# A hybrid attention and MLP step on 8 cores: staging of late input tiles, exponentials over two key tiles of both maps, and score bursts in halves

## The chip, the cores and the metric

One Trainium2 chip, a program on all 8 of its cores. Each core works on its own part: two prompts of 256 tokens and one half (1024 tokens) of a latent sequence of 2048, whose keys and values it computes in full. The metric is the device time in microseconds of the slowest core.

## The reference

One layer, run over context tokens (modulated by c_ctx) and latent tokens (modulated by c):

```
h = rms_norm(x) * (1 + scale) + shift          # scale, shift from silu(c) @ w_ada
q, k, v, u, g = split(h @ w_in)                # 1024 columns each
q, k = rms_norm per 64 (and rotary, latent tokens only)
a = softmax(q1 k1^T / 8) - lam * softmax(q2 k2^T / 8)   # 8 heads, two maps each
att = rms_norm(a @ v);  sgu = gelu(u) * (w_s @ layer_norm(gelu(g)) + b_s)
y = x + g1 * (concat(att, sgu) @ w_o)
y = y + g2 * (relu(h2 @ w_ff1)^2 @ w_ff2)      # h2: modulated norm of y
```

Context queries see the 256 keys of their own prompt; latent queries see 2048 latent keys and 256 cached ones. The keys and values of the context tokens are outputs too.

## The kernel before, in words

A core has 12 tiles of 128 tokens of its own (0 to 3 context, 4 to 11 latent) and 8 tiles (12 to 19, "late") of the other half of the sequence, which need only keys and values. Heads are handled in pairs, p = 0 to 3.

**How the order is made.** The program is written by a planner (class Sched). Work is described by generators ("threads") with priorities; a small model of the engines' costs, of PSUM banks and of the DMA rate decides when each posted operation is issued, and that order becomes the fixed order of each engine's instructions. Semaphore waits are added from the data dependences alone. So an event (Ev), a pool (Pool) or a delay in the planner sets where an instruction stands in its engine's queue; on the chip it then waits only for its data. A lower number is a higher priority.

**Start.** Modulation weights (ada, 8 units u of 4 parts) stream in through POOL's DMA queue, with weights of the projections and the input tiles x. norm_x(tt) squares a tile on ACT, takes the inverse root, scales it into xn and gives its x buffer back. The projections of the own tiles for pair 0 (k, q, v) and pair 1 (v) are summed in four quarters of the contraction as the modulation becomes known: 24 units, VU (12 of v) and KU (12 of k and q), whose partial sums live in SBUF. When the last quarter of a KU unit is added, chain_qk normalises it, applies the rotary (rope_in, on DVE and POOL) and writes it to one of 8 buffers kr; a DMA transpose on SP's queue then writes it to KT or QT of the pair. `drained` fires when a partial sum is dead.

**Late tiles.** loads0 loads them in order, each from the pool named in xpool; staging() gives the buffers as memory comes free. Buffer 0 is given at once, buffer 1 when VU[:4] have drained, 4 and 5 (at p1) when KU[:4] and KU[4:8] have. late_group(t0) transposes two tiles on PE (identb) into PSUM, modulates them into hO and gives their xn buffers back; group_ev[t0] fires. half_free says when the parts of hO, which overlap x buffers 0 and 1, may be written. After the 24 units proj0 projects k and v of the four late groups, late_v1 the v of pair 1 (weights wr, input hO).

**Attention.** attention(p) goes over 152 items (a head, 256 queries, one key tile) in 38 bursts of four. For each item two maps of 64 rows: K of the map is the weight or moving operand of a 64-row matmul, and the two maps use the two halves of the array. Map m, item j has the columns m * 1024 + j * 256 of PSUM banks 0 to 3, so banks 0 and 1 hold map 0 and banks 2 and 3 map 1. Two exponentials, one per map, 128x1024 each, read them into a tile P. One token Stok is held from the burst until both are done. av() multiplies P with V (VV, with a column of ones) into banks 4 and 5; finalize() divides, subtracts, normalises and stores to attd. Attention has priority 10; the projections of the next pairs (30), the gates (32) and others fill PE between the bursts, through the two free banks. Attention of pair 0 starts when proj_end[0], all xnev and QTev[0][0] have fired. Events per pair: sc_end (last scores posted and their tokens passed), av_done, att_end (finalised). The chains of pair p >= 2 wait for att_end[p - 2] before they write KT, QT or VV. For pair 0 the planner adds 8 us (TURN_SLACK) to each transpose.

**After attention**: the rest of the gates, the u units with the spatial mixing, the output projection, norm, and eight rounds of the MLP, all on PE without a break.

Lines of the profile are those of the helpers: L455 matmuls, L465 transposes on PE, L488 activations, L498 the inverse root (two ACT instructions), L510 tensor_tensor, L517 tensor_scalar, L543 a scaling on POOL, L549 scalar_tensor_tensor, L558 copies, L562 reductions, L586 loads, L591 stores, L597 DMA transposes.

Of the kernel before, what the change touches and what calls it, by code (L numbers as in the profile page):

```python
# [9 lines left out]
F32 = mybir.dt.float32  # L10
# [5 lines left out]
D = 2048  # L16
# [4 lines left out]
K = 1024  # L21
# [8 lines left out]
PE_SWITCH = 100.0  # L30
DMA_RATE = 315.0
# [591 lines left out]
def build_program():  # L623
# [113 lines left out]
    xt = [S.sbuf("xt%d" % i, [128, D], F32, b) for i, b in enumerate((SB + 86 * K, SB + 78 * K, slot1 + 17408, z1 + 4 * K, p1, p1 + 8 * K))]  # L737
    xts = Pool(S, range(4))
    xta, xtb, xtp = Pool(S), Pool(S), Pool(S)
    xpool = [xts] * 12 + [xta, xtb, xta, xtb, xtb, xta, xta, xtp]  # L740
    xn = [S.sbuf("xn%d" % i, [128, D], BF16, slot1 + i * 4 * K) for i in (2, 3, 0, 1)]
    xns, xno = Pool(S, range(4)), Pool(S)
# [34 lines left out]
    sc_ev, ident_ev, const_ev, tab_ev, lam_ev = Ev(), Ev(), Ev(), Ev(), Ev()  # L777
    own_x, ho_free, slot1_ev, wr2_ev, ada_out = Ev(), evs(4), Ev(), Ev(), Ev()
# [66 lines left out]
    def staging():  # L845
        xta.give(0)
        yield [drained[k] for k in VU[:4]]
        xtb.give(1)
        yield [drained[k] for k in KU[:4]]
        xtp.give(4)  # L850
        yield [drained[k] for k in KU[4:8]]
        xtp.give(5)
        yield [drained[k] for k in KU[8:]]
        xno.give(2)
        xno.give(3)
        yield xnev[12:20] + [group_ev[18]]
        slot1_ev.fire()
# [41 lines left out]
    def ada0():  # L899
        yield [sc_ev, const_ev]  # L900
        for u in range(8):
# [5 lines left out]
            yield op  # L907
            yield S.copy(mod0, bank(j))
# [77 lines left out]
    def chain_qk(b, kind, t0, p, op):  # L986
# [74 lines left out]
        yield att_end[p - 2 if p >= 2 else 4]  # L1061
        if p == 1:
            yield slot1_ev
        yield S.turn(dst[:, t0:t0 + 2].rearrange("p t h n -> p (t h) n"), zn, "kr%d" % kj)
# [45 lines left out]
    def chain_v(b, t0, p, op):  # L1110
        s = p % 2
        yield [op, att_end[p - 2 if p >= 2 else 4]]
# [15 lines left out]
    def cached(p):  # L1128
        s = p % 2
        yield att_end[p - 2 if p >= 2 else 4]  # L1130
# [10 lines left out]
        VVev[p][10].fire()  # L1141
        yield S.turn(KT[s][:, 20:22].rearrange("p t h n -> p (t h) n"), kr[kj], "kr%d" % kj)
# [83 lines left out]
    def half_free(h):  # L1226
        yield [drained[k] for k in VU[4 * h + 4:4 * h + 8]] if h < 2 else xnev[12:17] if h == 2 else xnev[12:19]
# [84 lines left out]
    Stok, Otok = Pool(S, [0]), Pool(S, [0])  # L1312
# [25 lines left out]
    def attention(p):  # L1338
        s = p % 2
        yield [sc_end[p - 1], QTev[p][0], tab_ev]  # L1340
        if p == 0:
            yield [proj_end[0]] + xnev
# [13 lines left out]
        def av():  # L1356
            yield av_done[p - 1]
            n = 0
            while n < len(items):
# [24 lines left out]
                n += len(its)  # L1384

        av_end = S.spawn(av(), 10.5)
        for i0 in range(0, len(items), 4):
# [3 lines left out]
            yield Stok  # L1391
            n = len(its) * 256
# [6 lines left out]
            yield S.mm(ops, mode="row", cost=len(its) * 112.0)  # L1399
# [513 lines left out]
```

How the kernel before makes its waits and increments, by code:

```python
    def add(self, eng, fn, reads=(), writes=(), key=None, dr=(), dw=()):  # L204
# [63 lines left out]
            for s, v in nd.snap.items():  # L268
                if known.get(s, 0) < v:
                    known[s] = v
            known[nd.sem] = nd.val
        E = self.eng[eng]
        wl = list(waits.items())
        attach = None
        if eng != "pe" and wl:
            attach = wl.pop()
        for s, v in wl:
            E.wait_ge(self.sems[s], v)
        ins = fn(E)
        if attach:
            ins._wait_ge(self.sems[attach[0]], attach[1])
        nd = Node()
        nd.eng = eng
        nd.dma = dma
        if dma:
            name = "d_" + key
            if name not in self.sems:
                self.sems[name] = self.nc.alloc_semaphore(name)
                self.dcnt[name] = 0
            self.dcnt[name] += 1
            ins.then_inc(self.sems[name], 16)
            nd.sem, nd.val = name, 16 * self.dcnt[name]
        else:
            self.cnt[eng] += 1
            ins.then_inc(self.esem[eng], 1)
            nd.sem, nd.val = "c_" + eng, self.cnt[eng]
        nd.snap = dict(known)
        i = len(self.nodes)
# [301 lines left out]
    def wait_all_stores(self, keys):  # L600
        for k in keys:
            nd = self.nodes[self.dlast[k]]
            if self.known["sp"].get(nd.sem, 0) < nd.val:
                self.nc.sync.wait_ge(self.sems[nd.sem], nd.val)
```

## Time and profile before

| | us |
|---|---|
| median of 3 runs | 2464.01 (2458.88 to 2472.96) |
| the profiled execution's own time | 2466.38 |
| its span on the slowest core (core 4) | 2465.3 |
| spans of the 8 cores | 2444.4 to 2465.3 |
| PE busy | 2366.6 (96% of the span) |
| DVE busy | 1120.7 |
| ACT busy | 729.1 |
| POOL busy | 232.5 |

Busy time of PE is the union of its matmuls. "PE ps L465 <- ACT st L498" means that a transpose on PE waited for an instruction of line 498 on ACT. A row of a timeline gives start, duration, engine, line, operation, output and inputs, the number of merged instructions, and in brackets the idle time before. PEclk is the granted TensorE clock as a share of full speed.

### The profile page before, as it was taken

Reading aid. Unit: us, or ns where it says so; the run is one execution under the profiler, and the core shown is the slowest. Engines: PE = TensorE matmul, PEld = TensorE weight load, DVE = VectorE, ACT = ScalarE, POOL = GpSimd, SP = SyncE. Lnnn points to the kernel's source line nnn. Section 1 sums busy time; section 2 is a strip of 40 time slices with the busy share of each in tenths; the row PEclk is TensorE's granted clock in tenths of the full one; section 3 lists DMA queues with packets and bytes.
Section 4 is the critical chain, followed back from the end, with each engine's and each line's share of the span. In section 5 each row is a group of like instructions: output and inputs, shape, how many; then the busy total and the mean of one; then the engine's idle time right before and its main releaser. Section 6 shows DMA issues by size and latency. Waiting matters only on the chain.

```text
span 2465.3 us, 38569 instructions; the slowest of 8 cores (2444.4 to 2465.3 us)
## 1 busy us (share of the span) xinstructions
PE 2366.6 (96%) x16224; PEld 1357.6 (55%) x16224; DVE 1120.7 (45%) x2216; ACT 729.1 (30%) x1196; POOL 232.5 (9%) x394
## 2 busy tenths in 40 slices
PE   3689799999999999999999999999999999999999
PEld 2568687878888854444444444444444444444444
DVE  2567776744742154554101332322524616528347
ACT  2515576766756561222231001001010010010110
POOL 1213311111111030000110000000000000000000
PEclk9799899999999999999999999999999999999999
DMA  9995978967754285976563333333433434434346
GB/s 217 191 170 139 120 97 90 128 95 111 117 85 85 45 125 134 241 210 129 93 108 52 52 52 52 52 52 52 90 65 60 89 55 71 80 51 84 63 96 187
DMA packets 168729, 251.58 MB, mean 102 GB/s; under 512 B 101104, under 2 KB 106864, under 8 KB 154480
## 3 DMA queue, kind: packets, MB, share of 16 engines
q0 software_dynamic: 54816, 169.14, 42.3%
q1 hardware_dynamic: 113744, 79.97, 14.0%
q8 instruction: 132, 2.16, 0.4%
q14 instruction: 37, 0.30, 0.0%
HBM read 348.28 MB, written 32.67 MB: 155 GB/s over the span
## 4 chain that ended last, share of the span: by engine, by line
PE 91%; DMA 5%; DVE 2%; ACT 1%; issue 0%; POOL 0%; SPq 0%
PE ps L455 91%; DMA ada<-wa 2%; DMA QT<-kr 1%; DMA sk<-t 1%; DMA xt<-xp 1%; PE ps L465 1%; DMA wr<-wa 1%; DVE hT L517 0%; DVE xn L517 0%; DMA tab<-rsin 0%; ACT xn L488 0%; DMA sv<-t 0%; DVE t L510 0%; ACT hO L488 0%; POOL xn L543 0%
## 5 line engine op out<-in xcount | busy, mean ns | idle before, releaser
L455 PE MATMUL ps<-wf,aT 128*128 128x512 bf16 x3072 | 665.0, 379 | 0.0
L455 PE MATMUL ps<-hT,wf 128*128 128x512 bf16 x3072 | 665.0, 379 | 0.0
L455 PEld LDWEIGHTS ps<-wf,aT 128*128 128x128 bf16 x3072 | 300.3, 98 | 362.3 <-issue 0.8
L455 PEld LDWEIGHTS ps<-hT,wf 128*128 128x128 bf16 x3072 | 300.2, 98 | 362.4 <-issue 0.8
L488 ACT ACTIVATE tm<-ps 128x512 f32<-128x512 f32 x192 | 114.4, 597 | 1030.0 <-PE ps L455 1030.0
L510 DVE TENSOR_TENSOR aT<-tm 128x512 bf16<-128x512 f32 x192 | 132.7, 692 | 549.3 <-ACT tm L488 546.5
L455 PE MATMUL ps<-wr,hT 128*128 128x256 bf16 x2880 | 356.7, 280 | 19.6 <-DVE hT L517 15.8
L488 ACT ACTIVATE P<-ps 128x1024 bf16<-128x1024 f32 x304 | 296.5, 1020 | 148.6 <-PE ps L455 148.5
L455 PEld LDWEIGHTS ps<-wr,hT 128*128 128x128 bf16 x2880 | 280.8, 100 | 70.5 <-issue 33.9
L510 DVE TENSOR_TENSOR acc<-acc,ps 128x512 f32<-128x512 f32 x216 | 148.4, 687 | 154.2 <-PE ps L455 153.8
L455 PE MATMUL ps<-VV,P 128*128 128x129 bf16 x2432 | 166.0, 221 | 6.2 <-issue 3.3
L510 DVE TENSOR_TENSOR tm<-ps,g_t 128x512 f32<-128x512 f32 x168 | 115.9, 690 | 95.1 <-PE ps L455 94.9
L455 PEld LDWEIGHTS ps<-VV,P 128*128 128x128 bf16 x2432 | 141.8, 98 | 30.3 <-issue 29.7
L586 POOL DMA_DIRECT2D wf<-wf x64 | 33.9, 530 | 1185.1 <-PE ps L455 1150.7
L455 PE MATMUL ps<-wr,hO 128*128 128x256 bf16 x1024 | 121.3, 273 | 1.3 <-ACT hO L488 0.8
L455 PEld LDWEIGHTS ps<-wr,hO 128*128 128x128 bf16 x1024 | 97.2, 98 | 16.3 <-issue 5.8
L455 PE MATMUL ps<-QT,KT 64*128 64x256 bf16 x1216 | 93.2, 272 | 2.2 <-ACT P L488 1.8
L455 PE MATMUL ps<-hT,wu 128*128 128x512 bf16 x384 | 85.8, 379 | 0.0
L455 PE MATMUL ps<-wo,sguT 128*128 128x512 bf16 x384 | 84.8, 379 | 0.0
L510 DVE TENSOR_TENSOR acc<-acc,tm 128x512 f32<-128x512 f32 x120 | 82.9, 691 | 3.6
L586 POOL DMA_DIRECT2D wr<-wa x96 | 51.3, 551 | 297.2 <-PE ps L455 296.9
L465 PE MATMUL ps<-identb,xn 128*128 128x128 bf16 x320 | 30.3, 270 | 43.3 <-DVE xn L517 29.8
(177 smaller groups left out, 1610.9 us busy)
## 6 DMA issues: line engine op xcount, KB each, us to landing
wf<-wf POOLq DMA_DIRECT2D x64, 1024.0 KB, 9.9
wr<-wa POOLq DMA_DIRECT2D x96, 256.0 KB, 7.5
ada<-wa POOLq DMA_DIRECT2D x32, 512.0 KB, 22.0
xt<-xs POOLq DMA_DIRECT2D x16, 1024.0 KB, 8.8
x1d<-xw SPq DMA_DIRECT2D x12, 1024.0 KB, 5.7
x1b<-x1d SPq DMA_DIRECT2D x48, 256.0 KB, 3.0
wr<-wqkv POOLq DMA_DIRECT2D x44, 256.0 KB, 11.2
wo<-wo POOLq DMA_DIRECT2D x32, 256.0 KB, 9.9
```

The source lines that it names most:

```text
L455: ins = e.matmul(o, lhsT=l, rhs=r, start=st, stop=sp, skip_group_check=True)
L465: ins = e.transpose(o, i, ident)
L488: "act", lambda e: e.activation(out=out, in_=in_, func=func, bias=bias, scale=scale, **kw),
L510: return self.post(eng, cost, lambda: self.add(eng, lambda e: e.tensor_tensor(out=out, in0=a, in1=b, op=op), reads=[a, b], writes=[out]), ...
L586: eng, lambda e: e.dma_start(out=out, in_=src), writes=[out], key=key, dr=dr), 0, nbytes=nb, prio=prio)
```

## The change

**x buffers of the late tiles.** Buffers 4 and 5 at p1 are dropped; a new buffer 4 stands at b0, where the first two ada parts and later KT of pair 0 are. Two xn buffers (4 and 5) are added at b0 + 8 KB and b0 + 12 KB (ada parts 2 and 3; later the end of KT and most of QT of pair 0). All three are given when the last ada unit has been multiplied (ada_done). Tiles 12 to 19 now take buffers 0, 4, 1, 4, 0, 1, 4, 0 in place of 0, 1, 0, 1, 1, 0, 0, 4. half_free follows.

**Transposes of pair 0.** Those of keys of the own tiles wait in the planner for xnev[18], those of all queries, of the late keys and of the cached keys for group_ev[18]. Attention of pair 0 also waits for all KU units to be drained.

**Chains of pairs 2 and 3** wait for sc_end[p - 2] (KT and QT) or av_done[p - 2] (VV, cached) in place of att_end; the gates of context tokens wait for av_done[2]. av_done fires when the last product is done, no longer when it is posted.

**Exponentials and score bursts.** An exponential takes both maps of two items: 2 x 512 columns, from banks 0 and 2 or 1 and 3. Each half has a token of its own. When the first token is there and the second not, and the planner has under 600 ns of work on PE, queued and running, the burst is sent as two halves of four matmuls; otherwise it waits for both tokens and goes out whole.

```
--- before.py
+++ after.py
@@ -28,6 +28,7 @@
 PE_SWITCH = 100.0
+SPLIT = 600.0
 DMA_RATE = 315.0
@@ -734,11 +735,12 @@
     adas = Pool(S, range(NPART))
-    xt = [S.sbuf("xt%d" % i, [128, D], F32, b) for i, b in enumerate((SB + 86 * K, SB + 78 * K, slot1 + 17408, z1 + 4 * K, p1, p1 + 8 * K))]
+    xt = [S.sbuf("xt%d" % i, [128, D], F32, b) for i, b in enumerate((SB + 86 * K, SB + 78 * K, slot1 + 17408, z1 + 4 * K, b0))]
     xts = Pool(S, range(4))
-    xta, xtb, xtp = Pool(S), Pool(S), Pool(S)
-    xpool = [xts] * 12 + [xta, xtb, xta, xtb, xtb, xta, xta, xtp]
+    xta, xtb, xtc = Pool(S), Pool(S), Pool(S)
+    xpool = [xts] * 12 + [xta, xtc, xtb, xtc, xta, xtb, xtc, xta]
     xn = [S.sbuf("xn%d" % i, [128, D], BF16, slot1 + i * 4 * K) for i in (2, 3, 0, 1)]
+    xn += [S.sbuf("xn%d" % i, [128, D], BF16, b0 + (4 * i - 8) * K) for i in (4, 5)]
     xns, xno = Pool(S, range(4)), Pool(S)
@@ -775,6 +777,7 @@
     sc_ev, ident_ev, const_ev, tab_ev, lam_ev = Ev(), Ev(), Ev(), Ev(), Ev()
+    ada_done = Ev()
     own_x, ho_free, slot1_ev, wr2_ev, ada_out = Ev(), evs(4), Ev(), Ev(), Ev()
@@ -844,12 +847,12 @@
         xta.give(0)
+        yield ada_done
+        xtc.give(4)
+        xno.give(4)
+        xno.give(5)
         yield [drained[k] for k in VU[:4]]
         xtb.give(1)
-        yield [drained[k] for k in KU[:4]]
-        xtp.give(4)
-        yield [drained[k] for k in KU[4:8]]
-        xtp.give(5)
         yield [drained[k] for k in KU[8:]]
@@ -905,6 +908,8 @@
             yield op
+            if u == 7:
+                ada_done.fire()
             yield S.copy(mod0, bank(j))
@@ -1058,9 +1063,11 @@
         dst = QT[s] if kind == "q" else KT[s]
-        yield att_end[p - 2 if p >= 2 else 4]
+        yield sc_end[p - 2 if p >= 2 else 4]
         if p == 1:
             yield slot1_ev
+        if p == 0:
+            yield group_ev[18] if kind == "q" or t0 >= 12 else xnev[18]
         yield S.turn(dst[:, t0:t0 + 2].rearrange("p t h n -> p (t h) n"), zn, "kr%d" % kj)
@@ -1109,7 +1116,7 @@
         s = p % 2
-        yield [op, att_end[p - 2 if p >= 2 else 4]]
+        yield [op, av_done[p - 2 if p >= 2 else 4]]
         dst = VV[s][:, t0:t0 + 2, :, 0:128]
@@ -1127,7 +1134,7 @@
         s = p % 2
-        yield att_end[p - 2 if p >= 2 else 4]
+        yield av_done[p - 2 if p >= 2 else 4]
         if p == 1:
@@ -1139,6 +1146,8 @@
         VVev[p][10].fire()
+        if p == 0:
+            yield group_ev[18]
         yield S.turn(KT[s][:, 20:22].rearrange("p t h n -> p (t h) n"), kr[kj], "kr%d" % kj)
@@ -1224,7 +1233,7 @@
     def half_free(h):
-        yield [drained[k] for k in VU[4 * h + 4:4 * h + 8]] if h < 2 else xnev[12:17] if h == 2 else xnev[12:19]
+        yield [drained[k] for k in VU[4 * h + 4:4 * h + 8]] if h < 2 else xnev[12:18] if h == 2 else xnev[12:20]
         ho_free[h].fire()
@@ -1309,7 +1318,7 @@
     att_ev = [evs(8) for _ in range(6)]
-    Stok, Otok = Pool(S, [0]), Pool(S, [0])
+    Stok, Otok = [Pool(S, [0]), Pool(S, [0])], Pool(S, [0])
     O = [bank(4), bank(5)]
@@ -1339,7 +1348,7 @@
         if p == 0:
-            yield [proj_end[0]] + xnev
+            yield [proj_end[0]] + xnev + [drained[k] for k in KU]
             for i in range(3):
@@ -1382,36 +1391,41 @@
                 n += len(its)
+            yield op
 
             pj = yield Ps
-            yield Stok
-            n = len(its) * 256
+            yield Stok[0]
+            split = not Stok[1].free and S.backlog["pe"] + max(0.0, S.until["pe"] - S.now) < SPLIT
+            if not split:
+                yield Stok[1]
             ops = []
                                 QT[s][r, q0 // 128:q0 // 128 + 2, hh, :], True, True))
-            yield S.mm(ops, mode="row", cost=len(its) * 112.0)
-            es = [S.act(Pt[pj][:, m, 0:n], PS[:, m * 1024:m * 1024 + n], AF.Exp, scale=0.125) for m in range(2)]
-            left = [2]
-
-            def one():
-                left[0] -= 1
-                if left[0] == 0:
-                    Stok.give(0)
-            for e in es:
-                e.then(one)
+            if not split:
+                yield S.mm(ops, mode="row", cost=len(its) * 112.0)
+            es = []
+            for h in range(2):
+                if split:
+                    if h:
+                        yield Stok[1]
+                    yield S.mm(ops[4 * h:4 * h + 4], mode="row", cost=224.0)
+                e = S.act(Pt[pj][:, :, h * 512:(h + 1) * 512], bview(PS[:, h * 512:h * 512 + 1], ((1024, 2), (1, 512))), AF.Exp, scale=0.125)
+                e.then(lambda h=h: Stok[h].give(0))
+                es.append(e)
             todo.append((its, pj, es))
         if p == 3:
-            yield Stok
+            yield Stok[0]
+            yield Stok[1]
             for j in range(4):
@@ -1468,7 +1482,7 @@
             if t0 < 4:
-                yield att_end[2]
+                yield av_done[2]
             j = yield banks
                 for k0 in range(0, 16, 4):

```

## Rows read from the trace of the kernel before

**Rows 1.** The page: engine totals, then PE in 40 slices of the span (tenths).
```profile
PE 2366.6 (96%) x16224; PEld 1357.6 (55%) x16224; DVE 1120.7 (45%) x2216; ACT 729.1 (30%) x1196; POOL 232.5 (9%) x394
...
PE   3689799999999999999999999999999999999999
```

**Rows 2.** Busy time by stage: us, each engine busy (x instructions), PE clock, DMA share, GB/s.
```profile
0.00:180.00 180.00, 114.40 (x952) 87.73 (x952) 81.26 (x138) 56.87 (x93) 33.23 (x64) 0.91 1.00 191
180.00:287.50 107.50, 88.62 (x768) 75.36 (x769) 76.17 (x139) 59.71 (x127) 42.18 (x42) 0.87 0.66 129
287.50:849.00 561.50, 551.42 (x6733) 449.35 (x6734) 307.28 (x913) 373.72 (x571) 82.57 (x149) 0.99 0.67 97
```

**Rows 3.** PE's waits from 180 to 287.6 us: total, times, longest.
```profile
PE ps L465 <- ACT st L498: 6.2, 1, 6.2
PE ps L455 <- DMA wr<-wqkv: 3.4, 2, 2.4
PE ps L465 <- POOL xn L543: 3.2, 1, 3.2
PE ps L455 <- DVE hT L517: 2.7, 1, 2.7
```

**Rows 4.** PE's waits from 287.6 us to the end, same columns.
```profile
PE ps L455 <- DVE ot L549: 2.7, 1, 2.7
PE ps L455 <- ACT P L488: 1.8, 2, 1.1
```

**Rows 5.** Timeline of POOL's queue: start, us, what, idle before and its releaser.
```profile
164.92 0.58 POOL L586 DMA_DIRECT2D xt<-xs  x1
191.47 0.53 POOL L586 DMA_DIRECT2D xt<-xs  x1 [25.97 <-DVE VV L510]
...
239.34 0.53 POOL L586 DMA_DIRECT2D xt<-xs  x1 [0.60 <-DVE kr L510]
```

**Rows 6.** Timeline of ACT, norms of the first and the last late tile.
```profile
187.72 1.91 ACT L488 ACTIVATE xn<-xt 128x2048 bf16<-128x2048 f32 x1 [3.08 <-DMA xt<-xs]
...
255.87 2.00 ACT L488 ACTIVATE xn<-xt,st 128x2048 bf16<-128x2048 f32 x1
```

**Rows 7.** Timeline of PE: last ada weights, last late group, the first score burst.
```profile
179.26 0.40 PE L455 MATMUL ps<-ada,scT 128*32 128x512 bf16 x4 [1.17 <-DMA ada<-wa]
...
237.98 1.95 PE L465 MATMUL ps<-identb,xn 128*128 128x128 bf16 x32 [1.13 <-DVE xn L517]
...
258.13 3.41 PE L465 MATMUL ps<-identb,xn 128*128 128x128 bf16 x32 [6.24 <-ACT st L498]
...
287.51 0.61 PE L455 MATMUL ps<-QT,KT 64*128 64x256 bf16 x8 [0.38 <-DMA QT<-kr]
```

**Rows 8.** Timeline of SP's queue: the transposes of queries.
```profile
258.96 26.43 SPq L597 DMA_TRANSPOSE QT<-kr  x6
```

**Rows 9.** Timeline of PE in the middle of attention.
```profile
746.92 0.61 PE L455 MATMUL ps<-QT,KT 64*128 64x256 bf16 x8
747.46 1.08 PE L455 MATMUL ps<-VV,P 128*128 128x129 bf16 x16
748.38 1.91 PE L455 MATMUL ps<-wr,hT 128*128 128x256 bf16 x16
750.22 0.61 PE L455 MATMUL ps<-QT,KT 64*128 64x256 bf16 x8
```

**Rows 10.** Timeline of ACT in the same stretch.
```profile
747.57 1.94 ACT L488 ACTIVATE P<-ps 128x1024 bf16<-128x1024 f32 x2 [1.40 <-PE ps L455]
```

**Rows 11.** Timeline of PE after the last attention burst.
```profile
849.89 22.32 PE L455 MATMUL ps<-wr,hT 128*128 128x256 bf16 x203
```

**Rows 12.** Groups by shape on PE, 300 to 850 us: busy, mean ns, idle before.
```profile
L455 PE MATMUL ps<-wr,hT 128*128 128x256 bf16 x1974 | 239.1, 274 | 0.3 <-DVE S L510 0.3
...
L455 PE MATMUL ps<-QT,KT 64*128 64x256 bf16 x1192 | 91.4, 273 | 0.7 <-ACT P L488 0.7
L455 PE MATMUL ps<-wr,hO 128*128 128x256 bf16 x640 | 78.0, 273 | 0.0
```

## The prediction

> **What bounds the kernel now.** I read the page first: PE is busy in 96% of the span, and its slices are full but for the first eight or so [rows 1]. So time is won only where PE stands idle, or where it works at a low clock or switches its array mode more than it must. Second, the busy time by stage [rows 2], cut where the change acts: at 180 us the last ada weights are multiplied (a part at 179.26 [rows 7]) and at 287.5 the first score burst goes out. In those 107.5 us PE is busy for 88.62, at a mean granted clock of 0.87; in the 561.5 us with attention for 551.42, at 0.99. What comes before 180 the change leaves alone. Third, PE's waits in each stretch [rows 3, 4]: in the first, 6.2 us for a square root on ACT, 3.2 for a scaling on POOL (both the norm of a late tile), 3.4 for projection weights, 2.7 for the modulation; in the second, 2.7 for a finalisation and 1.8 in two waits for an exponential.
>
> The late tiles are followed through POOL's queue [rows 5]: tile 12 is issued at 164.92, tile 13 only at 191.47, after 26 us in which the queue waited for a v unit to drain, tile 19 at 239.34. On ACT the first is squared at 187.72 after waiting for its transfer, the last scaled at 255.87 [rows 6]; PE transposes the third pair at 237.98 and the last at 258.13 after 6.24 us idle [rows 7]. Then SP sends six transposes of queries in 26.43 us [rows 8], and the first burst goes at 287.51.
>
> **Part 1: late tiles earlier.** Removed is the wait of tile 13 for VU[:4]: its buffer is free when the last ada unit is multiplied, about 180, so its load can be issued some 11 us before 191.47. Three buffers turn round in place of two, and four xn buffers are there in place of two. The last tile was issued 48 us after tile 13. With three buffers, seven loads of 1 MB are left; if tile 12 lands at 187.7 and the others follow at the pace of the transfers (1 MB takes 8.1 us at the 129 GB/s of the stretch, 5.5 us at the 191 GB/s of the first 180 us [rows 2]), tile 19 lands between 226 and 244. With 5 us for its norm (252.9 landed, 257.9 done, the start and 2.00 us of the last scaling being in [rows 6]), it is ready between 231 and 249, where it was at 257.9. I take 240, between the ends, since DVE has 76.17 us and ACT 59.71 us of work in the stretch [rows 2] and norms queue behind them. The waits on norms then go: 6.2 + 3.2 + 1.1 (the idle at 237.98) = 10.5 us. The modulation's 2.7 and the weights' 3.4 stay: the weights start when the last late projection is done, earlier but no nearer to their use. Bounds: 0 (the planner counts on faster transfers than these and places the last transposes as much too early as now) and 15.4 (all waits but the 2.7 and some 0.8 for ada columns, out of 107.5 - 88.62 = 18.9 idle).
>
> **Part 2: the clock.** 128 of the 768 matmuls are transposes, 32 in 1.95 us [rows 7]; the others run at 22.32 / 203 = 0.110 us at full clock [rows 11]. That makes 640 x 0.110 + 128 x 0.061 = 78.2 us for work that took 88.62: 10.4 us go to the clock (0.87 on the mean, so part of the stretch ran at 1.2 GHz, the rest at 2.4) and to short gaps. With over half of the idle gone I take 4.5 back, bounds 0 and 10.4.
>
> **Part 3: transposes of pair 0 held back.** Keys of own tiles now go after tile 18 is normed, queries after group 18 is transposed. What is queued behind: SP's other work (stores, later transposes); the kr buffers, 8 of them, stay taken by six k and two q units, so the other q units and the late k chains wait, the latter with a PSUM bank each; and the first burst waits for the first q. Cover: after the 24 units PE has four groups of 96 matmuls of projection and 32 transposes, 4 x (96 x 0.110 + 2.0) = 50 us, which reach to about 184 + 22 + 50 = 256, and six plus three transposes at 26.43 / 6 = 4.4 us from 235 end at 275, before 287.5. I cost it at 0, with 0 and +20 as ends (rival 3).
>
> **Part 4: start of attention.** Between 287.5 and 300 PE waits 2.7 + 1.8 us [rows 4]. These depend on few queued projections; halves let a new burst start after one exponential. I take -2, bounds -4.5 and 0.
>
> **Part 5: splits and the form of the exponential.** A whole burst and its 16 products and 16 projection matmuls repeat in 3.30 us: 0.54 + 0.92 + 1.84 [rows 9]. The 64-row matmuls overlap in pairs (8 in 0.54 us is 0.068 each), and four pairs would take 4 x 0.110 = 0.44 of the 0.54; of the 1.84, 16 x 0.110 = 1.76 is work. So a change of mode there and back costs about 0.10 + 0.08 = 0.18 us, and a split adds one such pair. How often? From 300 to 850 us there are 1192 / 8 = 149 bursts and 1974 + 640 projection matmuls [rows 12], 17.5 to a burst, and each projection bank is posted as 32 at once, 3.5 us: the planner seldom has under 0.6 us queued. I take 12 splits, + 2 us; ends 0 and 152 x 0.18 = +27. The Trainium skill (TensorEngine Tiling (Array Packing), Key Properties) says that changing the tiling mode drains TensorE, which speaks against halves; by that rule every half sent is a loss, whatever waits it fills, and the sum would be +2 at 12 splits with no gain in part 4, so 2451. The trace bears the cost out, with 0.18 us for a pair of switches.
>
> The exponential keeps 1024 elements; two take 1.94 us [rows 10] from 747.57 to 749.51, and the next burst is at 750.22, so 0.7 us of slack hide up to 0.35 us more on each. The two-bank form is not in the trace; ends -0.1 and +0.35 us of each are both hidden, and I cost it at nothing. Where the slack is gone, each further 0.1 us costs up to 152 x 0.2 = 30 us.
>
> **Part 6: sc_end and av_done for att_end.** Chains of pairs 2 and 3 and caches start some microseconds earlier; PE's waits of 287.5 to 849 hold nothing that they could take away, so 0, ends -1 and +1 (order of PE's queue). After 849 PE is full [rows 1], and attention's end comes 22 us before the projections queued behind it run out [rows 11]: a shorter attention alone gives nothing.
>
> **Sum** against the profiled execution (span 2465.3, its time 2466.4): -10.5 - 4.5 + 0 - 2 + 2 + 0 = -15. The median of the runs is 2464.0, 2.4 below that execution: **2449 us**, 0.6% faster. A measurement of this kernel tells about 0.5% (12.3 us) from no change.
>
> **Rivals.** (1) *All gaps close*: 15.4 + 10.4 + 2 = 28 us, 2436. For: nothing between 180 and 256 lacks PE work. Against: DVE would be busy 76 of some 80 us. (2) *The tiles stay late*: the planner's order rests on faster transfers, PE sits at a transpose in order, or DVE sets the pace; gain 0 to 8, 2456 to 2464, say 2461. For: ACT waited for transfers of the first and last tiles, and 76.17 us of DVE leave little room. Against: two buffers forced a wait of 26 us that goes. (3) *A wait takes the place of another, slower*: SP's transposes of pair 0. If tile 18 is normed at 250 as now and nine to thirteen transposes at 4.4 us come first, the first burst is at 250 + 57 = 307 in place of 287.5, +19.5, less some 5 of waits that go: 2478. It decides if tile 18's norm ends after 287.5 - 9 x 4.4 = 248. Against: the first transposes took 1.2 us to issue and only the crowded ones 4.4. (4) *Splits where there is work*: halves go out in most bursts, or in none. At 152 splits +27, which with the other terms gives 2474; at none, 2447, part of the forecast. [Rows 12] speak against the first.
>
> **How the numbers follow.** Forecast 0.45 (its own range 2441 to 2456), rival 1 0.12, rival 2 0.30, rival 3 0.08, rival 4 0.05. The forecast's case lies partly within 12.3 us: of its 0.45 some 0.32 is beyond, and with rival 1 and a little of rival 2 faster is 0.48; same is 0.42 (the rest of both); slower is 0.10, from rivals 3 and 4 less what stays within bounds. The range takes in rival 1 whole, rival 2 and most of rival 3: 2434 to 2472.
>
> **What would show it.** Right: POOL issues the second late tile near 180 and the last by 225; PE's waits from 180 to the first burst are under 9 us with none over 4 on a norm; the clock there is over 0.92; the first burst is near 272; three-piece patterns of 3.3 us fill attention and fewer than 20 bursts go as fours; exponentials still 1.02 us. Wrong: PE waits over 5 us for a transpose of QT or KT, or a first burst after 287; more than 60 halves; exponentials over 1.35 us.

## The result and the profile after: 0.7% slower

The changed kernel takes 1.007 times what the kernel before takes, with a 95% interval of 1.0046 to 1.0094 (20 executions of each, 12 of the changed kernel's in the comparison); a second comparison, on another occasion, gave 1.0058, 1.0031 to 1.0086 (e12 below). The forecast was 2449 us, 0.6% faster. The medians of all runs, 2488.18 against 2473.07 us, hold executions in which a whole die was disturbed; the ratios leave them out, and so does all that follows.

The profiled execution of the changed kernel took 2468.11 us, its slowest core 2465.9, and the kernel before had 2465.3. So the two profiled executions hardly differ, and the loss seems to be nowhere. It is found by reading all cores. First, the spans of the changed kernel's eight cores:

```profile
core 0: 2462.0 us, clock 0.985
core 1: 2457.7 us, clock 0.988
...
core 6: 2466.0 us, clock 0.980
core 7: 2465.9 us, clock 0.985
```

Before, the eight were spread from 2444.4 to 2465.3 us; now they lie between 2457.7 and 2466.0. Their mean went from 2453.2 to 2462.5, up 9.3 us, though the slowest core stood still. A kernel is judged by its slowest core, but the mean of eight cores is the steadier number, and for the experiments both are given: the ratio of the runs' times, and the change in that mean over all compared runs of a kernel (its interval by drawing whole runs anew). The pair of profiles doesn't show all of the loss: of the changed kernel's compared executions three lie between 2464.6 and 2469.7 us, like the profiled one, and nine between 2476 and 2489. This upper bunch is taken up in the last section; e12 gives +15.7 us in the mean with it and +9.8 without the spans over 2470 us of either kernel. What follows here reads the lower bunch.

Second, the busy times of a fixed stretch, 180 to 360 us, on all cores (columns as in [rows 2]). Of eight rows each, the two ends of the kernel before, core 3 and core 5:

```profile
180.00:360.00 180.00, 156.09 (x1554) 130.00 (x1555) 128.25 (x275) 106.99 (x206) 53.27 (x60) 0.91 0.76 125
...
180.00:360.00 180.00, 164.75 (x1753) 137.88 (x1752) 138.87 (x309) 116.89 (x223) 55.44 (x64) 0.97 0.70 124
```

and those of the changed kernel, core 2 and core 6:

```profile
180.00:360.00 180.00, 158.21 (x1607) 133.75 (x1605) 141.98 (x275) 98.78 (x204) 69.87 (x64) 0.93 0.64 116
...
180.00:360.00 180.00, 153.13 (x1509) 129.72 (x1510) 135.22 (x269) 96.25 (x199) 68.98 (x61) 0.90 0.66 119
```

PE gets through 1656 matmuls here on the mean of the eight cores before, and through 1562 after. The 94 that are missing are worth up to 94 x 0.110 = 10.3 us, all of the 9.3 and a little more. (The price is that of a 128-row matmul; a 64-row one takes 0.068, so these sums are upper ends.) POOL has 15 us more to do (its norms). Cut finer, in means of eight cores: from 180 to 260 the changed kernel is ahead, 680 matmuls against 638; from 260 to 360 it does 884 against 1020, at a granted clock of 0.90 against 0.96; from 360 to 450, 1096 against 1128. So the early tiles gave up to 4.6 us, and then up to 15 + 3.5 us were lost where attention starts; some 48 of the 136 missing from 260 to 360 are 64-row ones.

Third, PE's waits on the slowest core, 180 us to the first score burst at 314 (columns as in [rows 3]):

```profile
PE ps L456 <- DVE kr L511: 9.6, 1, 9.6
PE ps L466 <- POOL xn L544: 7.0, 1, 7.0
PE ps L456 <- DMA wr<-wqkv: 3.7, 1, 3.7
PE ps L456 <- DVE hT L518: 2.7, 1, 2.7
```

and from there to the end of attention, 314 to 870 us:

```profile
PE ps L456 <- ACT P L489: 6.7, 10, 1.2
PE ps L456 <- ACT st L499: 1.1, 1, 1.1
```

The two waits on norms of [rows 3] (6.2 and 3.2) have become one of 7.0, now on POOL. A wait of 9.6 us on the work of DVE on a unit of keys is new; on the other seven cores it is 3.9 to 10.3 us, listed on kr or on t, the mean of all eight 6.9, and no core had it before. And the waits for exponentials went from 1.8 in two to 6.7 in ten [rows 4].

POOL's queue, with the late tiles (columns as in [rows 5]):

```profile
176.48 0.53 POOL L587 DMA_DIRECT2D xt<-xs  x1 [13.13 <-PE ps L456]
...
197.31 5.44 POOL L544 TENSOR_SCALAR xn<-xt,st 128x2048 bf16<-128x2048 f32 x1 [1.04 <-ACT st L499]
...
208.68 7.05 POOL L544 TENSOR_SCALAR xn<-xt,st 128x2048 bf16<-128x2048 f32 x1 [0.95 <-ACT st L499]
215.69 1.15 POOL L587 DMA_DIRECT2D xt<-xs  x2
219.34 5.97 POOL L544 TENSOR_SCALAR xn<-xt,st 128x2048 bf16<-128x2048 f32 x1
229.34 5.44 POOL L544 TENSOR_SCALAR xn<-xt,st 128x2048 bf16<-128x2048 f32 x1 [1.56 <-ACT st L499]
```

Tile 13 is issued at 176.48 in place of 191.47, the last at 215.7 in place of 239.34, and the last scaling, on DVE, ends at 237.0 (2.17 us from 234.86), 21 us earlier than the 257.9 of [rows 6]. The loads did all that was asked of them. But four scalings of late tiles are now on POOL, at 5.4 to 7.0 us each, where ACT takes 2.00 [rows 6] and the other four take 1.3 to 2.2 on DVE; before, one was on POOL, one on ACT and six on DVE. PE meets one of POOL's:

```profile
225.45 2.72 PE L466 MATMUL ps<-identb,xn 128*128 128x128 bf16 x24 [7.04 <-POOL xn L544]
...
300.78 1.04 PE L456 MATMUL ps<-wr,scT 128*32 128x256 bf16 x16 [9.59 <-DVE kr L511]
```

The second of these is the new stall. DVE's timeline has its cause, kr buffers that are not given back:

```profile
270.13 0.69 DVE L511 TENSOR_TENSOR kr<-ps,st 128x512 bf16<-128x512 f32 x1 [4.75 <-DMA QT<-kr]
275.35 0.69 DVE L511 TENSOR_TENSOR kr<-ps,st 128x512 bf16<-128x512 f32 x1 [2.74 <-DMA QT<-kr]
279.48 0.69 DVE L511 TENSOR_TENSOR kr<-ps,st 128x512 bf16<-128x512 f32 x1 [3.43 <-DMA QT<-kr]
287.74 0.69 DVE L559 CAST kr<-ps 128x512 bf16<-128x512 f32 x1 [5.70 <-DMA QT<-kr]
```

DVE works in order, so each new kr waits until one of the six query transposes has read an old one out, and what stands behind it on DVE waits too: 16.6 us in four steps. The kernel before knew this wait, but shorter; on its slowest core:

```profile
DVE kr L510 <- DMA QT<-kr: 5.2, 1, 5.2
```

On its eight cores DVE waits 0 to 7.9 us for a transpose, 3.3 in the mean; on those of the changed kernel 10.4 to 16.6, 11.9 in the mean. The query transposes themselves are as slow as before (26.6 us for six, [rows 8] has 26.4) and start no earlier: at 246.5 to 259.0 us before and at 252.0 to 258.1 now, though the last late tile is transposed on PE some 9 us earlier in the mean.

The first score burst comes at 307.1 to 314.5 us on the eight cores, before at 269 to 288. This alone costs little. On the slowest cores, up to that burst PE has done 960 + 1029 = 1989 matmuls now, and 952 + 768 = 1720 before [rows 2]: 269 more are 29.6 us of work, and the burst is 26.9 us later. Attention begins later because more projection is put ahead of it.

### The profile page after: what moved, and what is told of

It is laid out like the page before. It is cut to its first block, busy times and chain, and to the rows that moved or that the text cites. A ratio compares the mean times of both kernels' runs of the same rounds, so it can differ in the third digit from the quotient of the medians.

```text
span 2465.9 us, 38561 instructions; the slowest of 8 cores (2457.7 to 2466.0 us)
## 1 busy us (share of the span) xinstructions
PE 2366.6 (96%) x16224; PEld 1356.4 (55%) x16224; DVE 1120.1 (45%) x2209; ACT 730.3 (30%) x1201; POOL 248.7 (10%) x396
## 4 chain that ended last, share of the span: by engine, by line
PE 91%; DMA 3%; DVE 3%; ACT 2%; POOL 1%; issue 0%; SPq 0%; DVEq 0%; ACTq 0%
PE ps L456 91%; DMA ada<-wa 1%; ACT P L489 1%; DMA QT<-kr 1%; DMA xt<-xp 1%; POOL xn L544 1%; DVE t L511 0%; PE ps L466 0%; DVE kr L511 0%; DMA xt<-xs 0%; DVE xn L518 0%; DVE hT L518 0%; DMA tab<-rsin 0%; ACT xn L489 0%; DVE st L563 0%
## 5 line engine op out<-in xcount | busy, mean ns | idle before, releaser
L489 ACT ACTIVATE P<-ps 128x1024 bf16<-128x1024 f32 x304 | 296.5, 1020 | 135.6 <-PE ps L456 135.4
L456 PEld LDWEIGHTS ps<-QT,KT 64*128 64x128 bf16 x1216 | 47.2, 94 | 40.8 <-issue 36.1
```

The lines of the kernel that those rows point to most:

```text
L456: ins = e.matmul(o, lhsT=l, rhs=r, start=st, stop=sp, skip_group_check=True)
L489: "act", lambda e: e.activation(out=out, in_=in_, func=func, bias=bias, scale=scale, **kw),
```

## The experiments

Sixteen runs were made, in four groups (e1 to e4, e5 to e8, e9 to e12, e13 to e16); each group shares its runs of the kernel before. The second and the third ran on chips of their own, the first and the fourth on a third one, so a difference between groups is taken by way of each group's kernel before, and is less sure than one within a group. In what they are built from, *bursts* means parts 4 and 5, *hold* part 3, *pairs* the edit of e5, *ends* part 6.

| run | what it is | ratio, 95% | mean of cores, us, 95% |
|---|---|---|---|
| e12 | the change, again | 1.0058, 1.0031 to 1.0086 | +15.7, 12.3 to 18.8 |
| e1 | before + bursts | 1.0048, 1.0022 to 1.0073 | +8.7, 6.3 to 12.3 |
| e2 | the change - bursts | 1.0030, 1.0017 to 1.0043 | +9.2, 7.8 to 10.6 |
| e3 | before + hold | 1.0003, 0.9992 to 1.0014 | +2.8, 1.7 to 3.9 |
| e4 | the change - extra xn | 1.0034, 1.0024 to 1.0045 | +10.3, 9.2 to 11.4 |
| e5 | the change, pairs | 1.0028, 0.9994 to 1.0061 | +6.8, 3.9 to 9.7 |
| e6 | before + bursts, pairs | 1.0001, 0.9991 to 1.0011 | +0.5, -0.9 to 1.9 |
| e7 | the change - extra xn, pairs | 0.9984, 0.9964 to 1.0005 | -3.7, -5.3 to -1.9 |
| e8 | the change - POOL norms, pairs | 0.9996, 0.9966 to 1.0026 | +0.4, -1.4 to 2.4 |
| e9 | e7 - POOL norms (the order of e7) | 1.0006, 0.9972 to 1.0041 | -1.0, -4.6 to 2.4 |
| e10 | e7, tile buffer over q | 1.0017, 0.9981 to 1.0052 | +1.4, -2.2 to 5.6 |
| e11 | e6 + ends | 0.9971, 0.9947 to 0.9996 | -0.2, -2.4 to 1.8 |
| e13 | before + early tiles | 0.9990, 0.9976 to 1.0005 | +2.1, 0.9 to 3.3 |
| e14 | before + ends | 1.0005, 0.9995 to 1.0015 | -0.3, -1.5 to 1.1 |
| e15 | e16, whole bursts | 0.9974, 0.9962 to 0.9986 | -2.6, -3.9 to -1.3 |
| e16 | e7, again | 0.9980, 0.9970 to 0.9991 | -1.8, -3.0 to -0.8 |

**The change in two halves, and the hold alone.** e1 puts the new exponentials, the two tokens and the halves into the kernel before and nothing else; e2 is the change with the bursts of before. Of the diff, e1 has these lines and what belongs to them, and e2 has all but these:

```diff
+    Stok, Otok = [Pool(S, [0]), Pool(S, [0])], Pool(S, [0])
...
+            split = not Stok[1].free and S.backlog["pe"] + max(0.0, S.until["pe"] - S.now) < SPLIT
...
+                e = S.act(Pt[pj][:, :, h * 512:(h + 1) * 512], bview(PS[:, h * 512:h * 512 + 1], ((1024, 2), (1, 512))), AF.Exp, scale=0.125)
+                e.then(lambda h=h: Stok[h].give(0))
```

> The kernel before with the new exponentials and half bursts alone. Theory H (the loss comes from the held-back transposes of pair 0: kr buffers run out, DVE and PE stand, and attention starts late): ratio 0.998 to 1.002, PE's waits on ACT P at most 4 us, first burst at 287 or earlier as before. Rival B (bursts and the exponential's form cost the time): ratio 1.004 or more, with exponentials over 1.03 us or over 6 us of waits on ACT P.

> The changed kernel with the exponentials and the single token of before. Theory H: ratio 1.004 to 1.009, the same as the whole change, a first burst near 310 us and a PE wait of 4 to 10 us near 290 to 300 that ends on DVE (kr or t). Rival B: ratio 1.000.

The two halves lose 8.7 and 9.2 us in the mean of the cores: both lose, e2 less than was expected by its ratio and e1 against the theory that only staging does. Together they are 17.9, and the whole change has 15.7, but that isn't shown to be a sum: 40% of e12's spans are over 2470 us against 5% and 3% here, and without such spans the halves have 7.4 and 8.8 and the change 9.8. Part of the two losses then is the same time. e1's waits name its cause. Core 4, PE and then ACT, from the first burst on:

```profile
277.69 0.61 PE L456 MATMUL ps<-QT,KT 64*128 64x256 bf16 x8
278.23 1.05 PE L456 MATMUL ps<-wr,hT 128*128 128x256 bf16 x8
280.43 0.40 PE L456 MATMUL ps<-QT,KT 64*128 64x256 bf16 x4 [1.15 <-ACT P L489]
282.02 0.40 PE L456 MATMUL ps<-QT,KT 64*128 64x256 bf16 x4 [1.20 <-ACT P L489]
```

```profile
278.34 1.94 ACT L489 ACTIVATE P<-ps 128x1024 bf16<-128x1024 f32 x2 [6.40 <-PE ps L456]
280.86 1.02 ACT L489 ACTIVATE P<-ps 128x1024 bf16<-128x1024 f32 x1 [0.58 <-PE ps L456]
282.46 1.02 ACT L489 ACTIVATE P<-ps 128x1024 bf16<-128x1024 f32 x1 [0.58 <-PE ps L456]
```

The halves don't overlap with exponentials. PE's half waits for the exponential just before it, and the next exponential waits 0.58 us for the half: 1.6 us for each half, 3.2 for a burst. The exponential itself is as long as ever, 1.02 us. The scheduler has the reason. It records what an instruction touches in PSUM as a range of banks, from the first column to the last (L172 to L177; one line higher before):

```
        lo = ap.offset % row
        hi = lo + sum(st * (n - 1) for st, n in ap.ap[1:])
        return range(lo * size // 2048, hi * size // 2048 + 1)
```

The new exponential reads banks 0 and 2, or 1 and 3, and is taken to hold 0 to 2, or 1 to 3. So the half that writes banks 0 and 2 also waits for the exponential over 1 and 3, which it doesn't touch. The token was split in two, and this range tied the two together again.

e3 adds the waits of part 3 to the kernel before:

```diff
+        if p == 0:
+            yield group_ev[18] if kind == "q" or t0 >= 12 else xnev[18]
         yield S.turn(dst[:, t0:t0 + 2].rearrange("p t h n -> p (t h) n"), zn, "kr%d" % kj)
```

> The kernel before with only the holding back added (keys of own tiles wait for the norm of tile 18, queries and late keys for group 18). Theory H: slower, ratio 1.004 to 1.012, DVE waits on DMA QT<-kr for 10 us or more, first burst at 305 us or later. Rival S (the earlier tiles and their norms on POOL are what costs): ratio 0.999 to 1.002.

The ratio is 1.0003: in the slowest core's time the hold costs nothing, in the mean of the cores 2.8 us. My theory that the hold by itself makes the staging half slow fell here. DVE does wait for a query transpose here, 4.4 to 9.3 us at once on the eight cores, but PE has work meanwhile, and waits 2.6 us at most behind a key's chain.

**Pairs of adjacent banks.** The columns are laid out so that the two key tiles of a half, both maps, are in two adjacent banks, and a range tells the truth:

```diff
-                    ops.append((PS[:, m * 1024 + j * 256:m * 1024 + (j + 1) * 256], KT[s][r, kt, hh, :],
+                    c = j // 2 * 1024 + m * 512 + j % 2 * 256
+                    ops.append((PS[:, c:c + 256], KT[s][r, kt, hh, :],
...
-                e = S.act(Pt[pj][:, :, h * 512:(h + 1) * 512], bview(PS[:, h * 512:h * 512 + 1], ((1024, 2), (1, 512))), AF.Exp, scale=0.125)
+                e = S.act(Pt[pj][:, :, h * 512:(h + 1) * 512], PS[:, h * 1024:(h + 1) * 1024].rearrange("p (m n) -> p m n", m=2), AF.Exp, scale=0.125)
```

e5 is this in the change, e6 in e1. The traces show the order of PE's 16224 matmuls to be the same as without it, in both.

> The changed kernel with another place of the scores in PSUM: the first two items of both maps in banks 0 and 1, the other two in banks 2 and 3, so that each exponential reads one contiguous pair of banks. PE's order is the same. Theory F (the planner tracks a PSUM operand as the range of banks from its first to its last column, so the exponential over banks 0 and 2 is also tied to bank 1, and one over 1 and 3 to bank 2: each half burst waits for the exponential just before it): PE's waits on ACT P fall from 6.7 us to under 3, exponentials of halves run back to back, ratio 1.001 to 1.005. Rival M (it is the change of array mode that costs): nothing changes, waits stay at 6 to 7 us, ratio 1.006 to 1.008.

> The kernel before with the new exponentials and half bursts, the scores placed in bank pairs. Theory F: waits on ACT P fall from 8 us in e1 to under 4, ratio 0.998 to 1.001. Rival M: ratio 1.004 or more as in e1.

e6 is at +0.5 us where e1 is at +8.7, and e5 at +6.8 where e12 is at +15.7: 8.2 and 8.9 us. PE's waits on P, in all and in the mean of the cores, sink from 7.9 to 1.6 us and from 6.7 (the profiled execution of the change) to 0.9. That the dependence costs time is thus shown twice, with the same order of matmuls and the same 1.02 us for an exponential. Its size in the change is less sure, since e12 has far more spans over 2470 us than e5 (40% against 8%); without these it is 4.3 us there, and 6.0 from e1 to e6. In e5, PE's waits from 300 to 870 us hold one row on P, and halves now follow each other in 0.8 to 0.9 us in place of 1.6:

```profile
PE ps L456 <- ACT P L489: 0.9, 2, 0.5
```

```profile
314.36 0.39 PE L456 MATMUL ps<-QT,KT 64*128 64x256 bf16 x4
315.13 0.40 PE L456 MATMUL ps<-QT,KT 64*128 64x256 bf16 x4 [0.38 <-ACT P L489]
316.05 0.39 PE L456 MATMUL ps<-QT,KT 64*128 64x256 bf16 x4
316.96 0.40 PE L456 MATMUL ps<-QT,KT 64*128 64x256 bf16 x4 [0.52 <-ACT P L489]
```

With the bursts cured, 6.8 us are left to the staging half (5.5 without spans over 2470 us).

**The staging half.** e4 and e7 take the fifth and sixth xn buffer out, without and with pairs; queries are then not held, and keys wait for tile 18's norm (the tile buffer lies there):

```diff
-        xno.give(4)
-        xno.give(5)
...
-            yield group_ev[18] if kind == "q" or t0 >= 12 else xnev[18]
+            yield [] if kind == "q" else xnev[18]
```

> The changed kernel without the two extra xn buffers, and so without any wait of the query transposes; keys of pair 0 still wait for the norm of tile 18. Theory H: most of the loss is gone, ratio 0.998 to 1.003, DVE waits on QT<-kr under 6 us. Rival S: as slow as the change, 1.005 or more.

> e4 with the scores in bank pairs. Theory F: waits on ACT P fall from 13.6 us to under 6, ratio 0.998 to 1.001, the first version of the staging that does not lose. Rival M: 1.003 or more.

Against e5, of the same group, this is worth 10.5 us. Against e12 e4 is 5.4 lower, but nothing (+10.2 against +9.8) without spans over 2470 us. In e4 the waits on P are the most of all runs, 13.4 us in the mean; e7, with the same order of matmuls, has 1.8 and is 14.0 us lower. So the false dependence hid the gain in e4. The traces of e4 and e7 show one thing more: no norm of a late tile is on POOL, all eight scalings are on DVE. With four buffers the planner doesn't choose POOL, so e7 takes away both the buffers and the norms on POOL. e8 keeps the buffers and bars the late tiles' norms from POOL (an affine, which the planner gives to DVE or ACT, for the scale):

```diff
-            yield S.scale(xn[j], xt[b], st[:, 1:2])
+            yield S.affine(xn[j], xt[b], st[:, 1:2], None)
```

> The changed kernel with bank pairs and with the scaling of late tiles on ACT or DVE only. If the norms on POOL (5.4 to 7.0 us each, 4 of them) hold up the late groups: the 7.0 us wait of PE on POOL xn goes and the ratio is 0.002 to 0.004 below that of e5. If they are hidden or DVE becomes the hold-up: same as e5, with as long a wait on DVE or ACT in its place.

It is worth 6.4 us against e5. PE's wait on a POOL norm is gone, and a wait on ACT has come, of 5.1 to 18.7 us on the eight cores. On core 2 it is the longest, while DVE waits 5.43, 4.06 and 5.46 us for query transposes:

```profile
PE ps L456 <- ACT st L499: 18.7, 1, 18.7
```

So the norms on POOL cost (the planner's order changed with them, so the 6.4 us need not be theirs alone), and 4.1 us lie between e8 and e7, which gives up the two buffers and the hold of the queries as well. e9 does both edits, e10 is e7 with the tile buffer 9 KB further on, over queries, so that queries wait and most keys don't:

```diff
-... z1 + 4 * K, b0))]
+... z1 + 4 * K, b0 + 9 * K))]
...
-            yield [] if kind == "q" else xnev[18]
+            yield xnev[18] if kind == "q" or t0 >= 18 else []
```

> e7 with the scaling of late tiles on ACT or DVE only. If norms on POOL and the kr buffers that are held are two separate costs, this is the best yet: ratio 0.995 to 0.998. If DVE is what the start waits for, it is e7's ratio again, 0.998 to 1.001.

> e7 with x buffer 4 over QT and the last keys of pair 0 in place of over KT, so that the six key transposes of own tiles wait for nothing and the query transposes for the norm of tile 18. Theory K (kr buffers held back make DVE and PE stand): DVE's waits on QT<-kr and PE's wait on ACT kr and sq (3 to 4 and 2.8 us in e7) shrink by half, ratio 0.995 to 0.998. Rival: the stall hangs on how slowly SP's transposes land while weights load, and stays; ratio as e7, 0.998.

By their times neither is decided. Their compared runs fall in two bunches, e9's at 2451 and at 2472 to 2476 us, e10's at 2454 to 2459 and at 2474 to 2478; what the upper bunch is, the last section shows. The traces say more. In e9 all engines have e7's instructions in e7's order (core 4 was compared), since e7 had no norm on POOL that could be barred: e9 is e7 once more, and its expectation of a further gain had nothing to rest on. For e10 I expected the waits of e7 to shrink by half; they grew. DVE waits 10.4 to 17.8 us for transposes from 240 to 320 us (12.6 in the mean, 8.0 in e7) and PE 4.2 to 10.1 us for the chain of a key (7.4, against 4.5). So with early tiles, to hold queries stops DVE longer than to hold keys.

**Single parts, with the kernel before under them.** e11 adds part 6 to e6, and e14 to the kernel before; e13 has part 1 alone (three tile buffers and the early loads; only the keys wait). Part 6 is:

```diff
-        yield att_end[p - 2 if p >= 2 else 4]
+        yield sc_end[p - 2 if p >= 2 else 4]
...
-        yield [op, att_end[p - 2 if p >= 2 else 4]]
+        yield [op, av_done[p - 2 if p >= 2 else 4]]
```

> e6 with the chains of pairs 2 and 3 waiting for sc_end and av_done. I had costed this at 0: ratio as e6, 0.999 to 1.001. If it reorders PE's queue for the worse, 1.002 or more.

> The kernel before with the earlier ends alone (part 6): chains of queries and keys wait for the last score burst, v chains and caches for the last product. Theory 0 (worth nothing, as predicted; the ratio of 0.997 of the run with bursts, bank pairs and ends was chance among executions): spans of the cores on the mean within 1 us of before, ratio 0.999 to 1.001. Rival G (it gains): spans 3 to 8 us shorter on the mean, ratio 0.997 to 0.9985.

> The kernel before with the three tile buffers and the early loads (part 1) alone: no fifth and sixth norm buffer, bursts, exponentials and ends as before; only the key transposes of pair 0 wait, for tile 18's norm. Theory N (the two extra norm buffers send norms to POOL and tie up the rest of staging, the loads themselves gain): PE waits under 1 us for a POOL norm, the spans of the cores are on the mean 2 to 6 us below those of the kernel before, ratio 0.998 to 0.9995. Rival S (moving the tiles earlier is itself worth nothing or less on this chip, and what the earlier run without the extra buffers won came from the halves and the ends): spans on the mean equal or longer, ratio 1.000 to 1.003.

e13's edit:

```diff
-    xpool = [xts] * 12 + [xta, xtb, xta, xtb, xtb, xta, xta, xtp]
+    xpool = [xts] * 12 + [xta, xtc, xtb, xtc, xta, xtb, xtc, xta]
...
+        yield ada_done
+        xtc.give(4)
...
+        if p == 0:
+            yield [] if kind == "q" else xnev[18]
```

e11 looked like a gain of 0.3%. The mean of its cores, -0.2 us, said otherwise, and e14 settled it: the ends are worth nothing, 1.0005. In its group 7% of the spans of the kernel before are over 2470 us and 1% of e11's, and most of the 0.9971 comes from there: the executions of up to 2470 us alone have 2461.3 against 2462.2 in the mean, 0.9996. e13 is the surprise: the early tiles alone gain nothing, 0.999 with 1 inside the interval, and +2.1 us in the mean. In means of eight cores, PE does 722 matmuls from 180 to 260 us against 638, 9 us won, 1032 against 1020 from 260 to 360, and 1004 against 1128 from 360 to 450, where it is busy for 79.4 us and was for 89.2; the first burst has gone to 294 to 305 us. On its core 1, waits of 4.7 us on a kr (180 to 300 us) and 7.0 on exponentials (from 300) stand where the norms' waits were:

```profile
PE ps L456 <- DMA wr<-wqkv: 5.2, 3, 2.7
PE ps L456 <- ACT kr L489: 4.7, 1, 4.7
...
PE ps L456 <- ACT P L489: 7.0, 6, 1.6
```

**Whole bursts or halves, and a version that beats both.** e16 is e7 again, e15 is the same with `SPLIT = -1.0`, so that each burst goes out whole.

> The change without the extra norm buffers and with bank pairs again, beside the run with whole bursts. Theory N: spans of the cores on the mean 2 to 6 us below those of the kernel before, as in its first run (3.7), ratio 0.997 to 0.9995. Rival: the first run was chance, spans within 1 us of before, ratio 0.9995 to 1.001.

> The change without the extra norm buffers and with bank pairs, as in an earlier run, but every burst goes out whole (the threshold for a split is negative). Theory W (with adjacent banks the halves are worth next to nothing, since few bursts find the queue short): within 1.5 us of the run with halves of the same call, on the mean of the cores' spans. Rival V (halves fill waits at the start of attention): 2 to 5 us longer than that run, and PE's waits on P from the first burst to 330 us over 3 us, where the run with halves has under 2.

Both beat the kernel before, by 0.20% and 0.26%, and both beat the change. Halves save waits: P costs 5.9 us in five waits in e15 and 1.8 in three in e16. Yet e15 isn't slower (2.6 us under the kernel before in the mean, against 1.8). So halves, even without the false dependence, are worth nothing that these runs can tell. Of the kernels whose gain shows in both numbers e15 has the lowest ratio, though it isn't to be told from e16: early tiles, four norm buffers, pairs, ends, no halves.

> The changed kernel once more, beside the others: ratio 1.005 to 1.008 with waits of 6.7 us on ACT P, so that the experiments add up to it: bursts +0.0048, staging +0.003.

e12 stood beside e9 to e11 as a yardstick, and confirms the loss.

## Why the prediction was wrong, by its own steps

**Part 5, the form of the exponential, is the first step that failed.** I asked how long the two-bank form takes, bounded that, and costed it "at nothing". The duration was right: 1.02 us, no change. What I never asked is what the scheduler makes of the operand. The answer stood in code that the change doesn't touch, six lines that were there to be read, and it costs 8.2 us from e1 to e6 and 4 to 9 in the change (e5, e12). Splits were fewer than the 12 that I took: five, which show as ten groups of four, and at 0.18 us each they would cost 0.9 in place of 2. The rule of the Trainium skill (TensorEngine Tiling (Array Packing), Key Properties) that a change of tiling mode drains TensorE doesn't explain the loss either: e6 has the same switches as e1 and costs 0.5 us.

**Part 4 failed with it.** The 2 us that halves were to save at the start of attention came out as waits on P of 6.7 us where 1.8 had been. With the dependence cured they sank to 0.9, a gain of 0.9 over before. e15 and e16 differ by 4 us of such waits and not by their times, so that even these bring no time that the runs can tell.

**Part 1 had the mechanism right and the price wrong.** Issue at 180 (176.48), last tile by 225 (215.69), all as forecast; I took the last norm for 240 and it ended at 237.0. But the 10.5 us of waits on norms didn't go. 7.0 of them came back on POOL, an engine that I never priced for a norm, though the trace before had one such scaling on POOL, of 5.44 us, against ACT's 2.00. The extra buffers let the planner take POOL; e8 bars POOL and wins 6.4 us, e7 gives up the buffers and with them POOL's norms and the hold of queries, and wins 10.5. And e13, without them, still gives nothing: what is won by 260 us is given back after 360. This is what rival 2 held, with another reason than it had: the tiles were early, and the next waits, on kr and P, took over.

**Part 2 failed on the slowest core and on the others.** I took 4.5 us back and asked for over 0.92 up to the first burst; on the slowest core it is 0.90 from 180 to 314, where it was 0.87 up to its first burst. From 260 to 360 us it is 0.90 in the mean of the cores, against 0.96 before. The clock is down behind the stall on kr; the slowest core, 290 to 315 us:

```profile
290.00:315.00 25.00, 15.41 (x143) 12.64 (x142) 21.87 (x43) 8.99 (x25) 2.33 (x5) 0.80 0.54 98
```

**Part 3, costed at 0, is the step that rival 3 should have carried.** I named the mechanism (kr buffers held, chains waiting), and then took as cover that PE has 50 us of projection. PE was covered, but DVE is an engine in order: kr buffers that are still taken stop it for 16.6 us, where it was 5.2, and its late k chain stops PE for 6.9 us on the mean of the cores. e3 shows the limit of this: the hold alone costs 2.8 us in the mean and nothing on the slowest core. A stall of PE on the chain of a key stands in every run with early tiles: 2.5 to 5.3 us in e13 and 2.9 to 8.0 in e7, where only keys are held, and 3.9 to 10.3 in the change. So the hold of queries isn't its only cause, and that it comes from the hold together with early tiles is my reading; no run has early tiles and no hold. How the 6.8 us of e5 divide, beyond e7 and e8, isn't settled, since the planner's order changes with each edit. Rival 3 put the first burst at 307 (it is 307.1 to 314.5), but for the wrong reason: no transpose is waited for by the burst, and 269 more matmuls stand before it. "A first burst after 287" was a bad marker, since work that goes ahead of it isn't lost.

**Part 6 was right**: 0, by e14. The sign of the whole was wrong by two terms, 4 to 9 us for the dependence and 7 to 9 for staging (e5, e2), and none of the forecast gains of 15 shows in the time; the rest of the 0.7% is the upper bunch of the last section, which nothing in the prediction foresaw. Rival 4 priced halves too, by their number; five split bursts cost that much through how they wait, not through how many they are.

Not settled: why e7 and e16, which are e13 with pairs, bursts and ends, lie 4 to 6 us below it in the mean, though bursts and ends are worth nothing on the kernel before. Halves aren't the reason, since e15 has none and lies 4.7 us below e13 in the same group.

## What to carry to other kernels

When an edit gives an operand a new shape, read how the dependency tracker covers that shape before asking how long the instruction takes: a range over strided banks can undo the very split that the edit makes. A buffer that is held longer can be paid on the in-order engine that writes the next one, not on the engine that the buffer's data are for. And where eight cores run the same program, compare the mean of their spans too: the slowest core hid a loss of 9 us in one pair of profiles and showed a gain of 0.3% in e11 that wasn't there. A mean has its own trap, a second bunch of spans that one group has more of than another. And before an edit is run on top of another, see in the trace whether it still changes anything: e9 ran e7's program.

## What was not expected of the hardware

In 40% of the spans of single cores in e12's compared runs a core took over 2470 us, and in 7% of those of the kernel before in the same group. e12's profile caught two such cores, 4 and 5, with 2484.6 and 2483.9 us, next to core 6 with 2455.9. Two stretches of 20 us, core 4 and then core 6:

```profile
280.00:300.00 20.00, 8.96 (x87) 7.33 (x85) 14.61 (x28) 3.65 (x11) 0.39 (x1) 0.78 0.75 69
...
420.00:440.00 20.00, 20.00 (x222) 15.51 (x220) 11.38 (x30) 12.69 (x22) 2.13 (x4) 0.81 0.49 75
```

```profile
280.00:300.00 20.00, 7.42 (x68) 5.87 (x66) 15.52 (x31) 6.23 (x18) 2.16 (x4) 0.74 0.68 92
...
420.00:440.00 20.00, 20.00 (x255) 16.50 (x255) 11.03 (x28) 14.74 (x22) 2.12 (x4) 1.00 0.48 88
```

Both of these had a stretch with PE busy for less than half of 20 us; core 5 had none so empty (12.78 us from 280 to 300). Core 6 is back at the full clock by 340 us; cores 4 and 5 are at 0.81 from 340 until about 460 us with PE busy for 99 of the last 100 (a mean between the two levels of 1.2 and 2.4 GHz), and do 222 matmuls in 20 us where core 6 does 255. From 300 to 460 us core 4 does 1596 matmuls and core 6 1841; at the 12.05 in a us that core 6 does in the last 100 us of it, the 245 missing are 20 us, about the distance between the bunches. Whether a deeper idle stretch makes this likelier isn't shown: core 6 idled more than core 4 and recovered, and e9 and e10, with less idle time there than the change, had it in 17% and 22% of their spans, the last group of runs in none. Nor does the program alone decide it: e7, e16 and e9 have the same instructions in the same order, and 3%, 0% and 17% of their spans are over 2470 us. The 17% is of the chip on which e12 ran too; whether the chip or something else of that group brings it isn't shown, nor why e12 has more than its neighbours.
